# Eight of the eleven down blocks of each feed-forward part by seven products in place of eight on half their columns

## The reference, cut to what matters

```
def _swiglu(h, w_gu, w_down):
    g, u = jnp.split(h @ w_gu, 2, axis=-1)
    return (jax.nn.silu(g) * u) @ w_down          # h 256 x 1024, hidden 256 x 2816, out 256 x 1024

x = x + 0.5 * _rmsnorm(_swiglu(_rmsnorm(x, ffn1_pre_g), ffn1_w_gu, ffn1_w_down), ffn1_post_g)
...
x = x + 0.5 * _rmsnorm(_swiglu(_rmsnorm(x, ffn2_pre_g), ffn2_w_gu, ffn2_w_down), ffn2_post_g)
```

## Time and profile before

| | |
|---|---|
| median of 3 runs | 1080.41 us (1080.12 to 1081.45) |
| the profiled execution | 1081.31 us, span 1079.4 us |
| PE (matmul) busy | 1068.7 us, 99% |
| DVE busy | 789.1 us, 73% |
| ACT busy | 608.5 us, 56% |
| DMA | 190.71 MB, mean 177 GB/s |

### The profile page before, as it was taken

The page is one execution under the profiler, slowest core; times in us unless marked ns, Lnnn a source line. Parts: engine busy times, 40 slices in busy tenths (PEclk is TensorE's granted clock), DMA queues, the critical chain, the costliest instruction groups (busy, mean ns, idle before and its releaser), DMA issues.

```text
span 1079.4 us, 21082 instructions
## 1 busy us (share of the span) xinstructions
PE 1068.7 (99%) x8534; PEld 1009.7 (94%) x8534; DVE 789.1 (73%) x1125; ACT 608.5 (56%) x905; POOL 0.2 (0%) x4
## 2 busy tenths in 40 slices
PE   9999999999999999999999999999999999999999
PEld 7999999999989999999999998999999799999898
DVE  5665556989979777778778555775655887997884
ACT  5544444678586545878445556444444575655471
POOL 0000000000000000000000000000000000000000
PEclk9999999999999999999999999999999999999999
DMA  9866556465543454444546533465556355542251
GB/s 343 292 213 211 176 182 209 151 221 174 179 154 121 152 181 157 157 164 149 208 166 244 196 106 130 147 230 198 188 182 212 119 177 200 191 157 95 102 196 39
DMA packets 29297, 190.71 MB, mean 177 GB/s; under 512 B 3656, under 2 KB 4521, under 8 KB 7466
## 3 DMA queue, kind: packets, MB, share of 16 engines
q1 hardware_dynamic: 26480, 182.53, 48.6%
q10 hardware_dynamic: 2746, 7.16, 1.9%
HBM read 188.62 MB, written 1.05 MB: 176 GB/s over the span
## 4 chain that ended last, share of the span: by engine, by line
PE 87%; DVE 9%; ACT 2%; issue 1%; DMA 1%; SPq 0%; DVEq 0%; ACTq 0%
PE bank L526 15%; PE bank L528 15%; PE bank L527 15%; PE bank L538 10%; PE bank L539 10%; PE bank L540 10%; DVE sb_w_lo L2098 3%; PE bank L625 2%; PE bank L761 1%; DVE sb_ssd_conv L2409 1%; DMA sb_w_raw<-in_w 1%; PE bank L709 1%; PE bank L886 1%; ACT sb_w_hi L1371 1%; PE bank L1048 1%
## 5 line engine op out<-in xcount | busy, mean ns | idle before, releaser
L2098 DVE TENSOR_TENSOR sb_w_lo<-sb_w_raw,sb_w_hi 128x2048 fp32r<-128x2048 f32 x169 | 386.4, 2289 | 118.9 <-ACT sb_w_hi L1371 118.5
L1371 ACT ACTIVATE sb_w_hi<-sb_w_raw 128x2048 fp32r<-128x2048 f32 x169 | 322.9, 1911 | 33.0 <-PE bank L528 29.2
L526 PE MATMUL bank<-sb_hT_hi,sb_w_hi 128*128 128x256 f32 (+1 forms) x816 | 225.7, 277 | 0.0
L528 PE MATMUL bank<-sb_hT_hi,sb_w_lo 128*128 128x256 f32 (+1 forms) x816 | 225.7, 277 | 0.0
L527 PE MATMUL bank<-sb_hT_lo,sb_w_hi 128*128 128x256 f32 (+1 forms) x816 | 225.6, 276 | 0.0
L538 PE MATMUL bank<-sb_hT_hi,sb_w_hi 128*128 128x256 f32 (+2 forms) x744 | 213.1, 286 | 0.2 <-DVE sb_hT_lo L2175 0.2
L539 PE MATMUL bank<-sb_hT_lo,sb_w_hi 128*128 128x256 f32 (+2 forms) x744 | 206.2, 277 | 0.0
L540 PE MATMUL bank<-sb_hT_hi,sb_w_lo 128*128 128x256 f32 x744 | 205.9, 277 | 0.0
L526 PEld LDWEIGHTS bank<-sb_hT_hi,sb_w_hi 128*128 128x128 f32 (+1 forms) x816 | 152.7, 187 | 0.0
L528 PEld LDWEIGHTS bank<-sb_hT_hi,sb_w_lo 128*128 128x128 f32 (+1 forms) x816 | 152.6, 187 | 0.0
L527 PEld LDWEIGHTS bank<-sb_hT_lo,sb_w_hi 128*128 128x128 f32 (+1 forms) x816 | 152.6, 187 | 0.0
(11 more groups left out here) (516 smaller groups left out, 2077.9 us busy)
## 6 DMA issues: line engine op xcount, KB each, us to landing
sb_w_raw<-in_w SPq DMA_DIRECT2D x169, 1024.0 KB, 4.9
sb_w_raw<-in_w SPq DMA_DIRECT2D x4, 512.0 KB, 7.8
sb_hT<-in_xT SPq DMA_DIRECT2D x2, 512.0 KB, 5.3
sb_x<-in_x SPq DMA_DIRECT2D x2, 512.0 KB, 11.8
sb_mem_xn<-in_mem ACTq DMA_DIRECT2D x1, 1024.0 KB, 7.1
sb_mem_T<-in_memT ACTq DMA_DIRECT2D x1, 1024.0 KB, 10.4
sb_post_g<-in_ffn_post_g ACTq DMA_DIRECT2D x2, 512.0 KB, 5.7
sb_decay<-in_c_decay ACTq DMA_DIRECT2D x1, 768.0 KB, 5.3
```

Of the source, the lines that this page charges most:

```text
L526: pe.matmul(o, a_hi, b_hi, start=first, stop=False)
L528: return pe.matmul(o, a_lo, b_hi, start=False, stop=last)
L1371: act.activation(w_hi[b % STAGES][:], w_raw[b % RING][:], ACT.Copy).then_inc(w_hi_in, 1)
L2098: tt(w_lo[b % STAGES][:], w_raw[b % RING][:], f32(w_hi[b % STAGES][:]), ALU.subtract).then_inc(w_lo_in, 1)
```

## The change

Let the hidden pair of a down block be A (two token halves by two tiles) and the right or left half of its weights B. For columns 512 to 1023 nothing changes: four products with 512 columns (`plain_half`, `last_product`). Columns 0 to 511 are cut into two halves of 256, so that A and B are both 2 x 2, and the four results are made from seven products with 256 columns in place of eight. The seven need sums of tiles and of weight quarters. DVE makes four sums of hidden tiles (`sum_raw`, 128 columns each) and three of weight quarters (`mix_raw`, 768 columns), ACT rounds them, DVE takes the rests. Two of the seven products are of no single output: they gather in banks 5 and 6, and are joined with the outputs once, after the eighth such block (`join`), ahead of the last two pairs. The down blocks 1 to 8 are made so; 0, 9 and 10 are as before. The order of quarters in those blocks is changed on the host. Banks 5 and 6 are opened by matmuls of zeros. `ffn_hi`, `ffn_lo`, `sum_hi` and `sum_lo` now begin 448 bytes into a 512-byte stretch of a partition; `ffn_hi` and `ffn_lo` began at a stretch's start before, and the weights still do.

```
-PAIR_TURNS = PAIRS - 3
+PAIR_TURNS = PAIRS - 4
...
-                "hi": place(24 + LINE, f"ffn{n}_hi", [P, 2, SEQ], F32R),
-                "lo": place(26 + LINE, f"ffn{n}_lo", [P, 2, SEQ], F32R),
+                "hi": place(24, f"ffn{n}_hi", [P, 2, SEQ], F32R),
+                "lo": place(26, f"ffn{n}_lo", [P, 2, SEQ], F32R),
...
+            def mixed_block(c, turn=0, parts=(512,), all_three=False):
...
+                    tile_in(c, 0, turn)
+                    plain_half(banks[7], 0, top)
+                    tile_in(c, 1, turn)
+                    plain_half(banks[7], 1, top)
+                    of_tile(5, 0, 0, top, hi, lo, b11, False)
+                    of_tile(3, 0, 1, top, hi, lo, b21, False)
+                    of_tile(4, 0, 1, low, mix_hi, mix_lo, u4, True)
+
+                    pe.wait_ge(S("ffn_sum_lo"), MIXED_PAIRS * (n - 1) + c + turn)
+                    of_sum(3, 1, 3, hi, lo, b22, True)
+                    of_sum(5, 1, 0, mix_hi, mix_lo, u1, True)
+                    of_sum(6, 0, 1, hi, lo, u2, False)
+                    of_sum(6, 1, 2, mix_hi, mix_lo, u3, True)
+                    plain_half(banks[last_bank], 0, low)
...
+                for q in range(n):                                   # open_banks, inside up block 3
+                        open_mixed(n, q)
+                        pe.matmul(banks[5 + q][:], zero_r[:], w[:, 0:512], start=True, stop=False)
...
             stay_warm(zeros[:, 0:P], zeros[:], 1)
+            open_mixed(1, 1)
+            pe.matmul(banks[6][:], zeros[:, 0:P], zeros[:], start=True, stop=False)
...
+                if b in MIXED_OF:                                     # ACT, round_block
+                    act.wait_ge(S("ffn_mixed"), MIXED_OF[b] + 1 + turn)
+                    act.activation(w_hi[b % STAGES][:], w_raw[b % RING][:], ACT.Copy)
+                    act.activation(mix_hi[:], mix_raw[:], ACT.Copy).then_inc(w_hi_in, 1)
...
+                def part_copies():                                    # ACT, ahead of join
+                    o = full(act, f"mixed{n}.0")
+                    act.activation(f["joined"][:, 0, 0:256], o[:, 0:256], ACT.Copy)
+                    copy(f"mixed{n}.0", f["parts"][:, 0, :], o[:, 256:512])
...
-                for i in range(4):                                    # ACT, squares at the end
-                    o = full(act, f"down{n}.{i}")
+                for m, i in enumerate((0, 2, 1, 3)):
+                    wait_read(act, f"down{n}.{i}")
+                    src = banks[fills[f"down{n}.{i}"][0]][:] if i % 2 else f["joined"][:, i // 2, :]
...
+                    ins = tt(mix_lo[:], mix_raw[:], f32(mix_hi[:]), ALU.subtract)   # DVE, low_block
...
+                tt(mix_raw[:, 0:512], quarter(0, 2), quarter(1, 3), ALU.add)        # DVE, mix_block
+                tt(quarter(1, 2), mix_raw[:, 0:256], quarter(2, 3), ALU.add)
+                tt(mix_raw[:, 512:768], quarter(1, 2), quarter(3, 4), ALU.add)
...
+                    mixed = 2 <= j < 2 * PAIRS - 4                    # DVE, hidden_tile
+                    if mixed:
+                        wait_read(dve, f"up{n}.{j}", turn)
+                        if j % 2:
+                            other_sums(j // 2, turn)
+                    for b in behind:
+                        if b in MIXED_OF:
+                            mix_block(b, turn)
...
-                for i in (1, 0, 3, 2):                                # DVE, after the last down block
+                for i in (0, 2):
+                    read(tt(y[:, i // 2, :], o[:], y[:, i // 2, :], ALU.add), key)
+                for i in (1, 3):
+                    read(gained(i, full(dve, key)[:]), key)
+                    scaled = gained(i - 1, y[:, (i - 1) // 2, :])
```

More of the change, by code:

```diff
@@ L143 @@
 BLOCKS = weight_blocks()
+MIXED_PAIRS = PAIRS - 3
 NBLOCK = len(BLOCKS)
@@ L148 @@
     FIRST.setdefault(_b[0], _n)
+MIXED_OF = {down_at(n, c): MIXED_PAIRS * (n - 1) + c - 1 for n in (1, 2) for c in range(1, PAIRS - 2)}
 COLS = {}
@@ L739, in up_block, with tile_in, last_product @@
                     feature_products(o, b, 2, hT_hi, hT_lo, key=f"up{n}.{j}").then_inc(block_done, 1)
-                def down_block(c, turn=0, parts=(512,), all_three=False):
+                def tile_in(c, k, turn):
+                    pe.wait_ge(S("ffn_lo"), FF_TILES * (n - 1) + 2 * c + 1 + k + 2 * turn)
+                def last_product(o, w_hi, w_lo, parts, all_three):
+                    t = slice(P, SEQ)
+                    for m, (a, w) in enumerate(((f["hi"], w_hi), (f["hi"], w_lo), (f["lo"], w_hi))):
+                        at = 0
+                        for width in parts if all_three or m == 2 else (512,):
+                            mm = pe.matmul(o[:, at:at + width], a[:, 1, t], w[:, at:at + width], start=False, stop=False)
+                            at += width
+                    return mm
@@ new lines, in open_banks, with plain_block @@
+                def open_banks():
+                    pe.wait_ge(S("zero_r"), n)
+                    w = w_hi[up_at(n, 3) % STAGES]
+                    for q in range(n):
+                        open_mixed(n, q)
+                        pe.matmul(banks[5 + q][:], zero_r[:], w[:, 0:512], start=True, stop=False)
+                def plain_block(c, parts=(512,), all_three=False):
+                    b = down_at(n, c)
+                    first, last = c == 0, c == PAIRS - 1
+                    pe.wait_ge(w_lo_in, b + 1 - SPLIT_FROM)
+                    hi, lo = halves(b, 2, D)
+                    if first:
+                        for i in range(4):
+                            claim(f"down{n}.{i}" if i % 2 else f"mixed{n}.{2 + i // 2}", down_banks[i],
+                                  None if i == 1 else down_at(n, PAIRS - 1 if i == 3 else PAIRS - 3))
+                    elif not last:
+                        for i in (0, 2):
+                            claim(f"down{n}.{i}", down_banks[i])
@@ L748, in down_block @@
                     for k in range(2):
-                        pe.wait_ge(S("ffn_lo"), FF_TILES * (n - 1) + 2 * c + 1 + k + 2 * turn)
-                        for i in range(4):
+                        tile_in(c, k, 0)
+                        for i in (0, 2, 1, 3) if last and k else range(4):
+                            o = banks[down_banks[i]]
                             t, h = slice(i // 2 * P, (i // 2 + 1) * P), slice(i % 2 * 512, (i % 2 + 1) * 512)
-                            first, last = c == 0 and k == 0, c == PAIRS - 1 and k == 1
-                            if k == 0 or i < 3 or len(parts) == 1:
-                                mm = product(o[i][:], f["hi"][:, k, t], f["lo"][:, k, t], hi[:, k, h], lo[:, k, h], first, last)
-                            else:
-                                for m, (a, w) in enumerate(((f["hi"], hi), (f["hi"], lo), (f["lo"], hi))):
-                                    at = 0
-                                    for width in parts if all_three or m == 2 else (512,):
-                                        cut = slice(i % 2 * 512 + at, i % 2 * 512 + at + width)
-                                        mm = pe.matmul(o[i][:, at:at + width], a[:, k, t], w[:, k, cut], start=False, stop=False)
-                                        at += width
-                            if c == PAIRS - 1 and k == 1 and i < 3:
@@ L764, in down_block @@
+                            if k and i == 3 and not last:
+                                mm = last_product(o, hi[:, 1, h], lo[:, 1, h], parts, all_three)
+                                continue
+                            mm = product(o[:], f["hi"][:, k, t], f["lo"][:, k, t], hi[:, k, h], lo[:, k, h],
+                                         k == 0 and (first or not last and i % 2 == 0), last and k == 1)
+                            if last and k == 1 and i < 3:
                                 ends(mm, f"down{n}.{i}")
@@ L2246, in hidden_tile @@
                         .then_inc(S("ffn_lo"), 1)
+                    if mixed:
+                        (sums_low if j % 2 else first_sum)(j // 2, turn)
                     for b in behind:
@@ L2275, in ffn_part @@
                 lowered[0] += 5 + TURN * PAIR_TURNS
+                b = lowered[0]
+                hidden_tile(FF_TILES - 4, [b], [b + 1], 0, [lambda: None, join])
+                hidden_tile(FF_TILES - 3, [], [b + 2])
+                lowered[0] += 3
                 b = lowered[0]
@@ L3103 @@
             at += m
+    for n in MIXED_OF:
+        top, low = stream[n, :, 0:1024].copy(), stream[n, :, 1024:2048].copy()
+        stream[n] = np.concatenate([top[:, 512:], low[:, 512:], top[:, 0:512], low[:, 256:512], low[:, 0:256]], axis=1)
     arrays["w"] = stream
```

148 lines of the change are left out of this document (124 added, 24 removed).

## The result

| | before | changed | ratio (95% interval) |
|---|---|---|---|
| median of 4 runs each | 1080.93 us | 1088.4 us (1087.26 to 1090.99) | 1.0072 (1.0055 to 1.009) |
| profiled execution, span | 1079.4 us | 1089.2 us | |

What follows compares the result with a forecast made beforehand. PE was taken to bound the kernel, with DVE's and ACT's chain nearly without slack in places. The terms summed to +2.4 on the profiled 1081.31 us, 1083.7 there, 1082.8 as a median; 8-in-10 range 1077.5 to 1087.5.

Steps and rivals of the forecast that it cites:

- The mixed block: PE in 16 down blocks: 21 matmuls of 256 columns replace 12 of 512, saving 0.275 us each, −4.4 us.
- longer pace: Rival, chance 0.10: up blocks behind mixed blocks run at 0.1178 us per matmul, not 0.1133; at most +6.9 us, 1088.5.
- Up 6 of part 1: Ahead of part 1's loop: DVE's added work delays up 6's low part, so PE waits +2.4 us.
- Part 2 ahead of the loop: Quarter sums on DVE, 1.6 us against 0.45 of slack, make PE wait +1.1 us.
- Opening matmuls: Three matmuls of zeros in the midst of PE's stream open banks 5 and 6: +0.7 us.
- Tile 21: At the join, DVE's additions make this tile late, so PE waits +0.6 us in part 1, +1.15 in part 2.
- The ends: Ends of the parts: more DVE operations and later ACT squares cost +0.9 us in part 1, +0.35 in part 2.
- The start: Program's start: an extra matmul of zeros keeps PE busy so the clock may rise sooner, −0.6 us.
- DVE's chain in the loop: A loop turn's chain takes about 15.7 us where PE takes 16.1: added work hidden, with a thin margin.
- DVE-bound loop: Rival, chance 0.08: the loop turn's chain is 16.5 us, not 15.7; 14 turns cost +5.6 us, 1088.
- Covered: Rival, chance 0.17: DVE's idle times take up work ahead of the loops, waits shrink from 6.7 to 1.5; about 1076.
- balance: Rival, chance 0.20: waits are half as large, 3.3 for 6.7 us, and the start gives −1.0; 1079.0 us.

Runs made afterwards that it cites:

- e1: The changed kernel with `ffn_hi` and `ffn_lo` put back to a stretch's start, the order of instructions unchanged; 1085.4 us.
- e3: The changed kernel with `ffn_hi`, `ffn_lo` and also `sum_hi`, `sum_lo` at a stretch's start; 1086.5 us.
- e6: The changed kernel with the sums at a stretch's start and each mixed block's last-bank products ahead of the four products of sums; 1085.4 us.
- e4: The changed kernel without the extra matmul of zeros at the program's start, bank 6 being opened within up block 3; 1089.5 us.
- e5: e1 with the norm of `mem` moved on DVE from ahead of part 1's loop to behind its third turn; 1087.4 us.

## Why the prediction was wrong, step by step

- **The mixed block, −4.4.** The size was right: 0.275 forecast, 0.28 in e1, 0.23 in the changed kernel. There it is lower because most of the block came in the pace of 0.1178, near an end of the range given.
- **Two up blocks at 10.90, unchanged.** This is the step that failed. It stood only in the rival "longer pace", at 0.10, and was held off with the pace of the loop before, at 0.1133. The rival's figure, 0.43 a turn, was right to 0.02: 14 loop turns × 0.41 = 5.7 us, which with the forecast's +2.4 makes 8.1 beside the 7.8 measured. That the two are so near is in part luck: tile 21 cost 1.45 less than forecast, because of these longer blocks, and other terms more. With the pace restored (e1) the kernel is still 4.5 us above the one before, not 2.4, for the stop at up 6 is then longer and both waits for tile 21 come up. The forecast had 0.1178 and 0.1133 before it and treated the pace as a property of a block and its operands. It is not: the block of the earlier trace rows itself runs at 0.1136 in the changed kernel, and the pace of the up blocks goes with what runs ahead of them, which the change altered. What sets it stays open.
- **Up 6 of part 1, +2.4.** 2.13 between the starts, less the 0.12 of a matmul: 2.0. In the order and for the reason given. Missed was that the clock can fall behind it, 1.5 us in this execution and in none of the three others: e1 and the changed kernel lost it behind stops of 2.46 and 2.13, e3, e6 and e4 kept it behind 2.38, 2.39 and 2.43.
- **Part 2 ahead of the loop, +1.1.** Two waits, of 600 and 577 ns between starts in place of 113 each: 0.95.
- **Opening matmuls +0.7.** 0.23 each, as forecast. In part 1 the 72 matmuls behind a single one are at 0.1178 besides, 8.48 us; behind two, in e4, they are at 0.1133 and take 8.18.
- **Tile 21, +0.6 and +1.15.** 0 and 0.3: the up blocks' loss covers it, since PE comes later. With the pace restored in e1 it is 0.5 and 1.3 by the starts, about the forecast's numbers. A wait and a pace don't add.
- **The ends, +0.9 and +0.35.** In part 1 1.50 us lie between the starts where 0.32 lay, 1.2 more, for +0.9 forecast and within its range; in part 2 it is 0.3, as forecast. The wait in part 1 by the changed kernel's trace:

```profile
209.34 0.39 PE L552 MATMUL bank<-sb_mem_hi,sb_w_hi 128*128 128x256 f32 x1 [1.23 <-DVE sb_w_lo L2220]
```

- **The start, −0.6, and zeros, +0.2.** Down 0 came 0.23 earlier, within 0.2 of the forecast, but for another reason (e4).
- **DVE's chain in the loop, 15.7.** 15.85, and hidden, as said, so the rival of a DVE-bound loop falls. What the forecast didn't draw from it is that a chain at 98% of PE's turn makes up little, 1.8 us in seven turns: most of what is late ahead of the loop is still late behind it (e1, e5).
- **Rivals.** Covered and balance fall with the waits found. The rule that only different row groups let loads overlap (the Trainium skill, TensorE: Matmul & The Clock Gate, Part 3, The mechanism) falls here: narrow matmuls with a load each start 0.1133 apart. The same section has a second case, a load into the background weight buffer, which the prediction left out.

## What to carry to other kernels

Where matmuls of one shape show two paces in one trace, a change that touches their neighbours can change the pace of blocks that it leaves alone: price that over all of them, and try the cut and the place apart, since each is one or two lines. A helper engine whose chain per turn is nearly as long as PE's turn is a second critical path, even when it is idle nearly a fifth of the time (DVE is busy 13.07 of e1's 16.11 us); look for its idle gaps and put other work into them in pieces no longer than the gap. The length of a stop of PE is not its whole price, for the clock may fall behind it.
